# Receptance projection in three fp32r passes, key units from one compact tile, decays taken shifted

## The chip, the cores and the metric

The kernel runs on one core of a Trainium2 chip. The metric is the device time of one execution in microseconds (us); shown are the median, the lowest and the highest of the runs.

## The reference, cut to what matters

The program computes two transformer blocks over 256 tokens of width 1024. The change lies in one stage of the second block, an RWKV-7 time mix with 16 heads of 64:

```python
xx = _token_shift(h) - h
xr, xw, xk, xv, xa, xg = [h + xx * mu[i] for i in range(6)]
r = (xr @ w_r).astype(f32)
k = (xk @ w_k).astype(f32)
v = (xv @ w_v).astype(f32)
w = -jax.nn.softplus(-(w0 + jnp.tanh(xw @ w1) @ w2).astype(f32)) - 0.5
a = jax.nn.sigmoid((a0 + (xa @ a1) @ a2).astype(f32))
g = jax.nn.sigmoid(xg @ g1) @ g2
kk = heads(k * k_k.astype(f32))
kk = kk / jnp.maximum(jnp.sqrt(jnp.sum(kk * kk, axis=-1, keepdims=True)), 1e-12)
k = k * (1.0 + (a - 1.0) * k_a.astype(f32))
decay = jnp.exp(-jnp.exp(w))
...
bonus = jnp.sum(rh * kh * r_k.astype(f32), axis=-1, keepdims=True) * vh
```

## The kernel before

Eight stages run one after the other, four of them feed-forward blocks (ffn) that take most of the span. All weights come as one stream of chunks of 128 x 2048 floats, 256 output columns of a matrix each, through three buffers (`raw`). A chunk is used in one of two ways. A plain chunk is multiplied as it is in fp32, 16 products of 128x256 (`plain_columns`, L986). A split chunk is rounded by ACT (ScalarE) to `whi` (`high`, L314), the rest `wlo` is made by POOL (GpSimd; `low`, L3372), and PE (TensorE) multiplies in three fp32r passes, 48 shorter products (`three_passes`, L341 to L343). The buffer of a plain chunk comes free when PE is done, that of a split chunk when its low part is made.

In the RWKV stage the receptance chunks are `RW(0)` to `RW(3)`, the keys `RW(4)` to `RW(7)`, the values `RW(8)` to `RW(11)`; of the first eight, 5 to 7 are split and the rest plain. DVE (VectorE) makes the six mixed inputs (`mix_tile`, L2534) into two homes, `variant_x[0]` and `[1]`, and the tile `x`. Variant 0 is for the keys, 1 and 2 for the decay and a LoRAs, 3 for the gate LoRA, 4 for the receptance, 5 for the values. Each engine runs its instructions in written order, tied by semaphores.

The order of PE is: keys 4 to 7 with a product that sums the squares of two key tiles behind each (`square_sums`, L2854; its output stands repeated over all 64 rows of a head, and the last one is between two LoRAs); the first halves of the LoRAs (`first`, L2847); their second halves (`second`, L2903), two and two, with the quarters of `RW(0)` between; `RW(1)` to `RW(3)` (L986); the values `RW(8)` (L999), in whose second half the bonus sums (L2928) wait for DVE's product `rk` (L2601); half of `RW(9)`; then the scores (L2962), which wait for the scaled factors. DVE divides the keys by their lengths in four steps (`unit_kk`, L2562 to L2564), then forms key and decay factors: running sums (L2582), a subtraction (L2584) that gives the sums before each token, and from ACT three exponentials (L2409, L2412, L2414).

## Time and profile before

| what | us |
|---|---|
| median of 3 runs | 1230.28 |
| lowest, highest | 1229.87, 1230.87 |
| the profiled execution, its own time | 1229.58 |
| its span | 1227.80 |
| what lies around the span | 1.78 |
| PE busy | 1215.9 |
| POOL, ACT, DVE busy | 778.8, 608.4, 539.5 |

Times in rows are us from the span's start. The RWKV stage lies from about 822 to 1020. An fp32 product stands in the trace as two records, an fp32r product as one. PE products overlap at their ends, so the pace of a row of them is read from start to start and not from the duration of one.

### The profile page before, as it was taken

The page shows a single profiled execution, that of the slowest core. Times are in us where ns is not written, and L with a number is a line of the kernel's source. Part 1 is how long each engine was busy: PE and PEld are TensorE (multiplying, and loading weights), DVE is VectorE, ACT ScalarE, POOL GpSimd, SP SyncE. Part 2 cuts the span into 40 slices and gives each one's busy share as a digit, 9 for nine tenths or more (in the row PEclk, how much of TensorE's full clock was granted, in tenths as well). Part 3 has the DMA queues.
Part 4 walks back from the last instruction along what each step waited for, and adds up shares of the span by engine and source line. Part 5 has one row for each costly group of instructions (what it writes and reads, how often), then busy time and mean ns, then how long its engine had stood idle before and what let it go on. Part 6 is the DMA issues. An engine that isn't in the chain of part 4 may idle for free.

```text
span 1227.8 us, 23237 instructions
## 1 busy us (share of the span) xinstructions
PE 1215.9 (99%) x9698; PEld 1060.6 (86%) x9698; DVE 539.5 (44%) x819; ACT 608.4 (50%) x796; POOL 778.8 (63%) x200
## 2 busy tenths in 40 slices
PE   8999999999999999999999999999999999999998
PEld 7888887788888888899998888888888998888887
DVE  4432234665433333243533332249996574332233
ACT  6544443545464444486465454455421445554443
POOL 3988880154288888766459888853015535888884
PEclk9999999999999999999999999999999999999999
DMA  7655554244255555554244555552342124555551
GB/s 295 212 196 191 185 202 152 74 177 164 78 194 208 177 199 182 194 197 172 94 144 175 204 176 201 180 196 104 119 156 71 37 74 169 179 199 196 181 203 70
DMA packets 31020, 202.01 MB, mean 165 GB/s; under 512 B 3424, under 2 KB 5344, under 8 KB 7392
## 3 DMA queue, kind: packets, MB, share of 16 engines
q1 hardware_dynamic: 28064, 196.63, 45.3%
q10 hardware_dynamic: 2880, 4.26, 1.1%
q8 instruction: 60, 0.98, 0.3%
q14 instruction: 16, 0.13, 0.0%
HBM read 198.79 MB, written 2.10 MB: 164 GB/s over the span
## 4 chain that ended last, share of the span: by engine, by line
PE 95%; POOL 1%; issue 1%; ACT 1%; DVE 1%; DMA 1%; SPq 0%; POOLq 0%; DVEq 0%
PE psum L353 25%; PE psum L355 13%; PE psum L344 10%; PE psum L346 10%; PE psum L345 10%; PE psum L986 6%; PE psum L999 3%; PE psum L2992 2%; PE psum L3008 1%; POOL wlo L3372 1%; PE psum L2847 1%; PE psum L341 1%; PE psum L343 1%; PE psum L342 1%; PE psum L2962 1%
## 5 line engine op out<-in xcount | busy, mean ns | idle before, releaser
L3372 POOL TENSOR_TENSOR wlo<-raw,whi 128x2048 fp32r<-128x2048 f32 x160 | 736.5, 4609 | 282.0 <-ACT whi L314 237.3
L353 PE MATMUL psum<-f_both,whi 128*128 128x512 f32 x1408 | 493.6, 394 | 2.0 <-DVE wlo L699 2.0
L314 ACT ACTIVATE whi<-raw 128x2048 fp32r<-128x2048 f32 x160 | 306.3, 1915 | 217.3 <-PE psum L355 169.5
L355 PE MATMUL psum<-f_both,wlo 128*128 128x256 f32 x1408 | 394.4, 280 | 0.0
L353 PEld LDWEIGHTS psum<-f_both,whi 128*128 128x128 f32 x1408 | 265.1, 188 | 60.9 <-DVE wlo L699 2.6
L355 PEld LDWEIGHTS psum<-f_both,wlo 128*128 128x128 f32 x1408 | 265.2, 188 | 1.5
L344 PE MATMUL psum<-whi,ahi 128*128 128x512 f32 x352 | 137.4, 390 | 0.2 <-POOL wlo L3372 0.2
L346 PE MATMUL psum<-whi,alo 128*128 128x512 f32 x352 | 137.0, 389 | 0.0
L345 PE MATMUL psum<-wlo,ahi 128*128 128x512 f32 x352 | 137.0, 389 | 0.0
L909 DVE TENSOR_TENSOR psum<-psum,arena 128x512 f32<-128x512 f32 x43 | 30.1, 700 | 237.3 <-ACT arena L625 237.2
L925 DVE TENSOR_TENSOR alo<-arena,ahi 128x512 fp32r<-128x512 f32 x44 | 99.6, 2264 | 31.7 <-ACT ahi L858 31.7
L916 DVE TENSOR_TENSOR psum<-psum,arena 128x512 f32<-128x512 f32 x44 | 30.8, 700 | 171.3 <-ACT arena L625 171.3
L344 PE MATMUL psum<-whi,hhi 128*128 128x256 f32 (+1 forms) x328 | 99.8, 304 | 0.8 <-POOL wlo L3372 0.6
L346 PE MATMUL psum<-whi,hlo 128*128 128x256 f32 (+1 forms) x328 | 97.0, 296 | 0.0
L345 PE MATMUL psum<-wlo,hhi 128*128 128x256 f32 (+1 forms) x328 | 96.9, 295 | 0.0
L344 PEld LDWEIGHTS psum<-whi,ahi 128*128 128x128 f32 x352 | 66.1, 188 | 14.3 <-POOL wlo L3372 0.5
L346 PEld LDWEIGHTS psum<-whi,alo 128*128 128x128 f32 x352 | 66.1, 188 | 13.9
L345 PEld LDWEIGHTS psum<-wlo,ahi 128*128 128x128 f32 x352 | 66.1, 188 | 12.1
L986 PE MATMUL psum<-arena,raw 128*128 128x256 f32 x320 | 73.9, 384 | 1.1 <-issue 1.1
L986 PEld LDWEIGHTS psum<-arena,raw 128*128 128x128 f32 x320 | 59.3, 190 | 10.7 <-issue 3.0
L344 PEld LDWEIGHTS psum<-whi,hhi 128*128 128x128 f32 x328 | 61.7, 188 | 5.0 <-issue 1.7
L858 ACT ACTIVATE ahi<-arena 128x512 fp32r<-128x512 f32 x44 | 27.9, 633 | 73.1 <-DVE arena L922 73.1
(425 smaller groups left out, 1506.7 us busy)
## 6 DMA issues: line engine op xcount, KB each, us to landing
raw<-stream SPq DMA_DIRECT2D x182, 1024.0 KB, 4.8
con<-consts SPq DMA_DIRECT2D x1, 1376.0 KB, 14.7
x<-x_in SPq DMA_DIRECT2D x1, 1024.0 KB, 5.1
raw<-stream SPq DMA_DIRECT2D x2, 512.0 KB, 7.5
kept_x<-x ACTq DMA_DIRECT2D x1, 1024.0 KB, 3.9
x<-kept_x ACTq DMA_DIRECT2D x2, 512.0 KB, 4.6
out<-x SPq DMA_DIRECT2D x4, 256.0 KB, 2.0
arena<-gm_w_s ACTq DMA_DIRECT2D x1, 512.0 KB
```

Of the source, the lines that this page charges most:

```text
L314: nc.scalar.activation(whi[:, slot, :], raw[:, c % RAW, :], ACT.Copy).then_inc(high_made, 1)
L344: nc.tensor.matmul(out, h_hi, w_hi, start=start, stop=False, skip_group_check=skip)
L345: nc.tensor.matmul(out, h_hi, w_lo, start=False, stop=False, skip_group_check=skip)
L346: return nc.tensor.matmul(out, h_lo, w_hi, start=False, stop=stop, skip_group_check=skip)
L353: nc.tensor.matmul(psum[:, bank, :].rearrange("p (a n) -> p a n", a=2), whi[w], f_both[:, :, k, :], start=k == 0, stop=False, skip_group_c ...
L355: return nc.tensor.matmul(psum[:, bank, 0:TOK], wlo[w], f_hi[:, k, :], start=False, stop=k == KT - 1, skip_group_check=True)
L909: nc.vector.tensor_tensor(left, left, aside[:, 0, :, :], ALU.add).then_inc(s("ffn_sum"), 1)
L916: nc.vector.tensor_tensor(left, left, aside[:, 1, :, :], ALU.add).then_inc(s("ffn_sum"), 1)
L925: nc.vector.tensor_tensor(flat(alo), act[:, b, :], flat(ahi).bitcast(F32), ALU.subtract)\
L986: mm = nc.tensor.matmul(psum[:, bank, j * 256:(j + 1) * 256], raw[:, slot, k * 256 + j * P:k * 256 + j * P + P], h[:, k, :], start=k == 0, ...
L999: mm = nc.tensor.matmul(psum[:, bank, m * 256:m * 256 + n], h[:, k, m * P:m * P + P], raw[:, slot, k * 256:k * 256 + n], start=k == 0, sto ...
L3372: nc.gpsimd.tensor_tensor(part(wlo[:, slot, :]), part(raw[:, c % RAW, :]), part(whi[:, slot, :]).bitcast(F32), ALU.subtract)\
```

## The change

The receptance chunks 1 to 3 become split chunks: ACT makes `whi` inside its own order (one in the middle of the sigmoids, two behind reads of `RW(0)` and `RW(1)`), DVE makes `wlo` (`receptance_low`), ACT and DVE also split variant 4 (`rx_hi`, `rx_lo`), and PE multiplies in three passes. The square sums are made by eight products with 32 output rows each into one bank (`square_sums`), one root, one clamp and one reciprocal follow, and eight products over 32 rows each spread the result (`spread_units`, behind `RW(1)`); DVE multiplies all keys in one instruction. Variants 1 and 2 are multiplied together, 64 output rows each (`first_pair`), variant 3 goes to the tile `x`. The subtraction and the first exponential go: the factor before each token is read one token to the left in the exponential of the running sums, within chunks of 64. The factor `r_k` moves from DVE's product into the weights of the bonus sums.

```diff
-RWKV_SPLIT = [("rw", 0, j) for j in (5, 6, 7)]
+RWKV_SPLIT = [("rw", 0, j) for j in (5, 6, 7, 1, 2, 3)]
...
+            rx_hi = below.enter_context(nc.sbuf_tensor("rx_hi", [P, KT, TOK], F32R))
...
+            rx_lo = below.enter_context(nc.sbuf_tensor("rx_lo", [P, KT, TOK], F32R))
...
-        mixed_x = lambda v: value_x if v == 5 else variant_x[v % 2]
+        mixed_x = lambda v: value_x if v in (3, 5) else variant_x[v % 2]
...
+        of_head = s3m[:, 256:384]
+        bonus_weights = s3m[:, 384:400].rearrange("p (k h) -> p k h", k=8)
...
+        def home_free(eng, v):
+            if v == 2:
+                eng.wait_ge(chunk_used, USE[CH[RW(4)]] + 1)
+                eng.wait_ge(s("rw_mixed"), 12)
+            if v == 3:
+                eng.wait_ge(s("x_kept"), 16)
+            if v >= 4:
+                eng.wait_ge(s("rw_first"), v - 2)
...
-            root(3)
+            eng.wait_ge(s("rw_sums"), 1)
+            nc.scalar.activation(roots[:, 0:2, :], bank2(2), ACT.Sqrt).then_inc(s("rw_root"), 1)
             eng.wait_ge(s("rw_first"), 2)
             nc.scalar.activation(lw[0:64, 0, :], psum[0:64, 0, 0:256], ACT.Tanh).then_inc(s("rw_lw"), 1)
             nc.scalar.activation(lw[64:128, 0, :], psum[64:128, 0, 256:512], ACT.Copy).then_inc(s("rw_lw"), 1)
+            for b in range(4):
+                k = slice(2 * b, 2 * b + 2)
+                eng.wait_ge(s("rw_mixed"), mixed(4, 2 * b + 1))
+                nc.scalar.activation(rx_hi[:, k, :], variant_x[0][:, k, :], ACT.Copy).then_inc(s("rw_rhi"), 1)
...
+                if k == 4:
+                    highs.upto(CH[RW(1)])
...
-                eng.wait_ge(s("rw_kx"), 4)
                 read(nc.scalar.activation(rr[:, 2 * j:2 * j + 2, :], bank2(proj_bank(name)), ACT.Copy), name)
-                if j == 0:
+                if j < 2:
+                    highs.upto(CH[RW(2 + j)])
+                if j == 1:
                     eng.wait_ge(s("rw_before"), 1)
-                    nc.scalar.activation(sw, sw, ACT.Exp, scale=-DECAY).then_inc(s("rw_exp"), 1)
-                if j == 1:
-                    eng.wait_ge(s("rw_before"), 2)
                     nc.scalar.activation(sw, sums, ACT.Exp, scale=DECAY).then_inc(s("rw_exp"), 1)
-                    eng.wait_ge(s("rw_exp"), 2)
+                    eng.wait_ge(s("rw_exp"), 1)
                     nc.scalar.activation(sums, sums, ACT.Exp, scale=-DECAY).then_inc(s("rw_exp"), 1)
...
+            for h in range(2):
+                steps(nc.vector.tensor_copy(of_head[:, 64 * h:64 * h + 64], const("block_ident", 32)[:, 16 * h:16 * h + 1].broadcast_to((P, 64))))
+            r_k = vec[:, VEC_AT["r_k"]:VEC_AT["r_k"] + 8].rearrange("p (k a) -> p k a", a=1).broadcast_to((P, 8, 2))
+            heads = const("same64")[:, 0:P:64].rearrange("p (a h) -> p a h", a=1).broadcast_to((P, 8, 2))
+            steps(nc.vector.tensor_tensor(bonus_weights, r_k, heads, ALU.mult))
...
+            for v in range(1, 5):
+                mix_variant(v)
+            eng.wait_ge(s("rw_root"), 1)
+            steps(nc.vector.tensor_scalar(roots[:, 0:2, :], roots[:, 0:2, :], 1e-12, None, ALU.max))
+            nc.vector.reciprocal(roots[:, 0:2, :], roots[:, 0:2, :]).then_inc(s("rw_unit"), 1)
+            mix_variant(5)
+            def receptance_low(j):
+                c = CH[RW(j)]
+                eng.wait_ge(high_made, LOWS[c] - 2)
+                eng.wait_ge(low_made, LOWS[c] - 1)
+                nc.vector.tensor_tensor(wlo[:, SLOT[c], :], raw[:, c % RAW, :], whi[:, SLOT[c], :].bitcast(F32), ALU.subtract)\
+                    .then_inc(low_made, 1)
+            for b in range(4):
                 k = slice(2 * b, 2 * b + 2)
-                eng.wait_ge(s("rw_kk"), 2 * b + 2)
-                steps(nc.vector.tensor_scalar(roots[:, k, :], roots[:, k, :], 1e-12, None, ALU.max))
-                steps(nc.vector.reciprocal(roots[:, k, :], roots[:, k, :]))
-                steps(nc.vector.tensor_tensor(kk[:, k, :], kk[:, k, :], roots[:, k, :], ALU.mult))
-            mix_variant(1)
-            unit_kk(0)
-            for v in (2, 3, 4):
-                mix_variant(v)
-            for b in range(1, 4):
-                unit_kk(b)
+                eng.wait_ge(s("rw_rhi"), b + 1)
+                nc.vector.tensor_tensor(rx_lo[:, k, :], variant_x[0][:, k, :], rx_hi[:, k, :].bitcast(F32), ALU.subtract)\
+                    .then_inc(s("rw_rlo"), 1)
+            receptance_low(1)
             eng.wait_ge(s("rw_sig"), 16)
             for k in range(8):
-                ins = nc.vector.tensor_scalar(rr[:, k, :], aa[:, k, :], 1.0, V_AT("k_a", k), ALU.subtract, ALU.mult)
+                ins = nc.vector.tensor_scalar(sums[:, k, :], aa[:, k, :], 1.0, V_AT("k_a", k), ALU.subtract, ALU.mult)
             steps(ins)
             for j in range(4):
                 k = slice(2 * j, 2 * j + 2)
-                nc.vector.scalar_tensor_tensor(out=kx[:, k, :], in0=rr[:, k, :], scalar=1.0, in1=kx[:, k, :],
+                nc.vector.scalar_tensor_tensor(out=kx[:, k, :], in0=sums[:, k, :], scalar=1.0, in1=kx[:, k, :],
                                                op0=ALU.add, op1=ALU.mult).then_inc(s("rw_kx"), 1)
+            receptance_low(2)
+            receptance_low(3)
+            eng.wait_ge(s("rw_kx"), 4)
             for k in range(8):
                 ins = nc.vector.tensor_tensor_scan(sums[:, k, :], const("restart", TOK), sw[:, k, :], 0.0, ALU.mult, ALU.add)
-            steps(ins)
-            nc.vector.tensor_tensor(sw, sums, sw, ALU.subtract).then_inc(s("rw_before"), 1)
+            ins.then_inc(s("rw_before"), 1)
             eng.wait_ge(S["rw_lw"], 6)
             nc.vector.tensor_tensor(gm_lo, lw[:, 1, :], gm_hi.bitcast(F32), ALU.subtract).then_inc(s("rw_lwlo"), 1)
             nc.vector.tensor_tensor(gt[64:96], lw[64:96, 2, :], gt[64:96].bitcast(F32), ALU.subtract).then_inc(S["rw_lwlo"], 1)
+            eng.wait_ge(s("rw_sums"), 2)
+            eng.wait_ge(s("rw_kk"), 8)
+            kk_halves = kk.rearrange("p (i g) t -> p i g t", i=2)
+            steps(nc.vector.tensor_tensor(kk_halves, kk_halves, psum[:, 2:6, :].rearrange("p g (i t) -> p i g t", i=2), ALU.mult))
             steps(nc.vector.tensor_tensor(aa, aa, kk, ALU.mult))
-            eng.wait_ge(s("rw_exp"), 1)
-            nc.vector.scalar_tensor_tensor(out=kk, in0=kk, scalar=-1.0, in1=sw, op0=ALU.mult, op1=ALU.mult).then_inc(s("rw_before"), 1)
-            eng.wait_ge(s("x_kept"), 16)
-            mix_variant(5)
+            chunks_of = lambda v: v.rearrange("p k (c t) -> p (k c) t", c=4)
             eng.wait_ge(s("rw_exp"), 2)
+            nc.vector.tensor_scalar(chunks_of(kk)[:, :, 0:1], chunks_of(kk)[:, :, 0:1], -1.0, None, ALU.mult)
+            steps(nc.vector.scalar_tensor_tensor(out=chunks_of(kk)[:, :, 1:64], in0=chunks_of(kk)[:, :, 1:64], scalar=-1.0,
+                                                 in1=chunks_of(sums)[:, :, 0:63], op0=ALU.mult, op1=ALU.mult))
             steps(nc.vector.tensor_tensor(aa, aa, sw, ALU.mult))
             for j in range(0, 4):
                 eng.wait_ge(bank_read[proj_bank(RW(j))], PROJ[RW(j)] // 2 + 1)
             eng.wait_ge(s("rw_kx"), 4)
             eng.wait_ge(s("rw_mixed"), mixed(5, 7))
-            for k in range(8):
-                nc.vector.scalar_tensor_tensor(out=rk[:, k, :], in0=rr[:, k, :], scalar=V_AT("r_k", k), in1=kx[:, k, :],
-                                               op0=ALU.mult, op1=ALU.mult).then_inc(s("rw_rk"), 1)
+            for k in (slice(0, 4), slice(4, 8)):
+                nc.vector.tensor_tensor(rk[:, k, :], rr[:, k, :], kx[:, k, :], ALU.mult).then_inc(s("rw_rk"), 4)
             eng.wait_ge(s("rw_rk"), 8)
             steps(nc.vector.tensor_tensor(kx, kx, sw, ALU.mult))
-            eng.wait_ge(s("rw_exp"), 3)
             steps(nc.vector.tensor_tensor(rr, rr, sums, ALU.mult))
             nc.vector.tensor_copy(pc, sums.rearrange("p k (c t) -> p k c t", c=4)[:, :, :, 63]).then_inc(s("rw_scaled"), 1)
...
+            def first_pair():
+                plain_loaded(eng, L0)
+                for k in range(KT):
+                    for v, h in ((1, 0), (2, 1)):
+                        eng.wait_ge(s("rw_mixed"), mixed(v, k))
+                        mm = nc.tensor.matmul(psum[head_rows(h), 0, h * 256:h * 256 + 256], raw[:, L0 % RAW, k * 256 + 64 * h:k * 256 + 64 * h + 64],
+                                              variant_x[v % 2][:, k, :], start=k == 0, stop=k == KT - 1)
+                return mm
+            def square_sums():
+                eng.wait_ge(s("rw_sq"), 8)
+                for half in range(2):
+                    for g in range(4):
+                        mm = nc.tensor.matmul(psum[32 * g:32 * g + 32, 2, half * 256:half * 256 + 256], const("same64")[:, 0:P:4],
+                                              roots[:, 4 * half + g, :], start=True, stop=True)
+                mm.then_inc(s("rw_sums"), 1)
+            def spread_units():
+                eng.wait_ge(s("rw_unit"), 1)
+                eng.wait_ge(s("rw_sig"), 16)
+                for half in range(2):
+                    for g in range(4):
+                        rows = slice(32 * g, 32 * g + 32)
+                        mm = nc.tensor.matmul(bank2(2 + g)[:, half, :], of_head[rows], roots[rows, half, :], start=True, stop=True)
+                mm.then_inc(s("rw_sums"), 1)
...
-            def split_by_tiles(slot, bank):
+            def split_by_tiles(slot, bank, h_hi=key_hi, h_lo=key_lo, made=lambda k: eng.wait_ge(s("rw_mixed"), 8 + k // 2 + 1)):
                 for k in range(KT):
-                    eng.wait_ge(s("rw_mixed"), 8 + k // 2 + 1)
+                    made(k)
                     for j in range(2):
                         w = (slice(None), slot, slice(k * 256 + j * P, k * 256 + j * P + P))
-                        mm = three_passes(bank2(bank)[:, j, :], whi[w], wlo[w], key_hi[:, k, :], key_lo[:, k, :], True,
+                        mm = three_passes(bank2(bank)[:, j, :], whi[w], wlo[w], h_hi[:, k, :], h_lo[:, k, :], True,
...
-                if j:
-                    square_sums(j - 1)
-            eng.wait_ge(s("rw_root"), 1)
-            first(1, 0, 0, L0, 0, P, 256).then_inc(s("rw_first"), 1)
-            square_sums(3)
-            first(2, 0, 1, L0, 0, P, 256).then_inc(s("rw_first"), 1)
-            eng.wait_ge(s("rw_root"), 2)
+            first_pair().then_inc(s("rw_first"), 2)
+            square_sums()
             first(3, 1, 0, L0, P, P, 256).then_inc(chunk_used, 1)
             first(3, 1, 1, L1, D, 96, 96).then_inc(s("rw_first"), 1)
             eng.wait_ge(s("rw_lw"), 2)
-            eng.wait_ge(s("rw_root"), 4)
+            eng.wait_ge(s("rw_root"), 1)
...
-                project(eng, RW(j), plain_columns, h=variant_x[0])
+                project(eng, RW(j), split_by_tiles, h_hi=rx_hi, h_lo=rx_lo, made=lambda k: eng.wait_ge(s("rw_rlo"), k // 2 + 1))
+                if j == 1:
+                    spread_units()
...
-                                          const("same64")[:, 0:P:64], start=True, stop=True)
+                                          bonus_weights[:, k, :], start=True, stop=True)
...
-                    elif c not in PLAIN and names[c] not in (("lora", 0, 2), ("rw_o", 0, 1)):
+                    elif c not in PLAIN and names[c] not in (("lora", 0, 2), ("rw_o", 0, 1), RW(1), RW(2), RW(3)):```

On PE, from the last key chunk to the LoRAs' second halves, before (L2854 square sums, L2847 `first`, L2903 `second`):

```order
L2854 MATMUL psum<-arena,con 128x512 [waits rw_sq]
L2847 MATMUL psum<-arena,raw 128x256 [waits rw_mixed,raw_loaded0,rw_root]
L2847 MATMUL psum<-arena,raw 128x256 [waits rw_mixed] x7
L2854 MATMUL psum<-arena,con 128x512 [waits rw_sq]
L2847 MATMUL psum<-arena,raw 128x256 [waits rw_mixed,raw_loaded0]
L2847 MATMUL psum<-arena,raw 128x256 [waits rw_mixed] x7
L2847 MATMUL psum<-arena,raw 128x256 [waits rw_mixed,raw_loaded0,rw_root]
L2847 MATMUL psum<-arena,raw 128x256 [waits rw_mixed] x7
```

And now (L2877 `first_pair`, L2886 `square_sums`, L2866 `first`):

```order
L2877 MATMUL psum<-arena,raw 64x256 [waits rw_mixed,raw_loaded0]
L2877 MATMUL psum<-arena,raw 64x256 [waits rw_mixed] x15
L2886 MATMUL psum<-arena,con 32x256 [waits rw_sq]
L2886 MATMUL psum<-arena,con 32x256 x7
L2866 MATMUL psum<-x,raw 128x256 [waits rw_mixed,raw_loaded0]
```

The sixteen full-width products of variants 1 and 2 have become sixteen half-width ones, and the four square sums (the first two stand ahead of these rows, behind `RW(5)` and `RW(6)`) one group of eight.

On DVE, from the sums of the decays to the product for the bonus, before:

```order
L2579 SCALAR_TENSOR_TENSOR arena<-arena 128x512 x3
L2582 SCALAR_TENSOR_TENSOR arena<-con,arena 128x256 x8
L2584 TENSOR_TENSOR arena<-arena 128x2048 [waits dve_step]
L2586 TENSOR_TENSOR alo<-arena,ahi 128x256 [waits rw_lw]
L2587 TENSOR_TENSOR ahi<-arena,ahi 32x256
L2589 TENSOR_TENSOR arena<-arena 128x2048
L2591 SCALAR_TENSOR_TENSOR arena<-arena 128x2048 [waits rw_exp,dve_step]
L2534 SCALAR_TENSOR_TENSOR x<-arena,vec 128x256 [waits rw_first,x_kept]
L2534 SCALAR_TENSOR_TENSOR x<-arena,vec 128x256 x7
L2595 TENSOR_TENSOR arena<-arena 128x2048 [waits rw_exp]
L2601 SCALAR_TENSOR_TENSOR arena<-arena,vec 128x256 [waits bank_read6,bank_read7,rw_kx,rw_mixed,dve_step]
```

And now (L2579 is `receptance_low`, L2609 the keys times their units, L2622 the product for the bonus):

```order
L2579 TENSOR_TENSOR wlo<-raw,whi 128x2048 [waits low_made,high_made] x2
L2600 SCALAR_TENSOR_TENSOR arena<-con,arena 128x256 [waits rw_kx]
L2600 SCALAR_TENSOR_TENSOR arena<-con,arena 128x256 x7
L2603 TENSOR_TENSOR alo<-arena,ahi 128x256 [waits rw_lw]
L2604 TENSOR_TENSOR ahi<-arena,ahi 32x256
L2609 TENSOR_TENSOR arena<-arena,psum 128x2048 [waits rw_kk,rw_sums]
L2610 TENSOR_TENSOR arena<-arena 128x2048 [waits dve_step]
L2613 TENSOR_SCALAR arena<-arena 128x32 [waits rw_exp,dve_step]
L2614 SCALAR_TENSOR_TENSOR arena<-arena 128x32x63
L2616 TENSOR_TENSOR arena<-arena 128x2048 [waits dve_step]
L2622 TENSOR_TENSOR arena<-arena 128x1024 [waits bank_read7,bank_read6,rw_kx,rw_mixed,dve_step]
```

The running sums now stand behind two low parts of receptance chunks, and the mixing of the values has moved out to a place ahead of them.

On ACT, where the receptance is read, now (L2413 reads a projection, L317 is `high`, L2418 and L2420 the exponentials):

```order
L2413 ACTIVATE arena<-psum 128x512 [waits chunk_used]
L317 ACTIVATE whi<-raw 128x2048 [waits chunk_used,raw_loaded1]
L2413 ACTIVATE arena<-psum 128x512 [waits chunk_used]
L317 ACTIVATE whi<-raw 128x2048 [waits chunk_used,raw_loaded2]
L2418 ACT_TABLE_LOAD
L2418 ACTIVATE arena<-arena 128x2048 [waits rw_before]
L2420 ACTIVATE arena<-arena 128x2048 [waits rw_exp]
L2413 ACTIVATE arena<-psum 128x512 [waits chunk_used] x2
```

The high part of `RW(3)` stands behind the read of `RW(1)`, and the reads of `RW(2)` and `RW(3)` behind both exponentials.

## Rows read from the trace of the kernel before

**Rows 1.** The page: busy time of PE; the chain that ended last, by engine.

```profile
PE 1215.9 (99%) x9698; PEld 1060.6 (86%) x9698; DVE 539.5 (44%) x819; ACT 608.4 (50%) x796; POOL 778.8 (63%) x200
PE 95%; POOL 1%; issue 1%; ACT 1%; DVE 1%; DMA 1%; SPq 0%; POOLq 0%; DVEq 0%
```

**Rows 2.** Waits of PE, 822 to 1000: total us, times, longest; the longest.

```profile
PE psum L613 <- DVE arena L468: 0.6, 1, 0.6
```

**Rows 3.** Timeline, PE, 840 to 905: start, us, what, idle before.

```profile
840.55 1.02 PE L2854 MATMUL psum<-arena,con 128*128 128x512 f32 x2
841.16 0.19 PEld L341 LDWEIGHTS psum<-key_hi,whi 128*128 128x128 f32 x1 [0.42 <-POOL wlo L3372]
...
853.54 1.02 PE L2854 MATMUL psum<-arena,con 128*128 128x512 f32 x2
854.40 3.62 PE L2847 MATMUL psum<-arena,raw 128*128 128x256 f32 x16
...
858.71 10.52 PE L2847 MATMUL psum<-arena,raw 128*128 128x256 f32 x48
869.16 2.00 PE L2903 MATMUL psum<-arena,raw 64*128 64x256 f32 x16
...
876.67 24.44 PE L986 MATMUL psum<-arena,raw 128*128 128x256 f32 x112
900.95 3.64 PE L999 MATMUL psum<-raw,x 128*128 128x256 f32 x16
904.42 0.50 PE L2928 MATMUL psum<-con,arena 128*128 128x2 f32 x4
```

**Rows 4.** Timeline, PE, mix1 stage: products narrower than 128, side by side.

```profile
241.06 0.75 PE L1705 MATMUL psum<-arena 32*32 32x32 f32 x64
...
308.80 1.97 PE L1779 MATMUL psum<-arena 128*64 128x128 f32 x32
```

**Rows 5.** Timeline, DVE, 836 to 903.

```profile
836.17 11.97 DVE L2534 SCALAR_TENSOR_TENSOR arena<-arena,vec 128x256 f32<-128x256 f32 x8
...
883.90 4.76 DVE L2582 TENSOR_TENSOR_SCAN arena<-con,arena 128x256 f32<-128x256 f32 x8
888.70 2.29 DVE L2584 TENSOR_TENSOR arena<-arena 128x2048 f32<-128x2048 f32 x1
...
896.34 3.25 DVE L2534 SCALAR_TENSOR_TENSOR x<-arena,vec 128x256 f32<-128x256 f32 x8
...
902.07 3.25 DVE L2601 SCALAR_TENSOR_TENSOR arena<-arena,vec 128x256 f32<-128x256 f32 x8 [0.28 <-DVE arena L2595]
```

**Rows 6.** Groups by line and shape, DVE: count, busy us, mean ns.

```profile
L1417 DVE TENSOR_TENSOR hlo<-arena,hhi 128x2048 fp32r<-128x2048 f32 x1 | 2.2, 2248 | 0.0
...
L1519 DVE TENSOR_TENSOR arena<-arena 128x1024 f32<-128x1024 f32 x1 | 1.2, 1226 | 0.0
```

**Rows 7.** Timeline, ACT, 853 to 902.

```profile
853.74 0.84 ACT L2375 ACTIVATE arena<-psum,vec 128x256 f32<-128x256 f32 x2 [3.95 <-PE psum L343]
...
870.58 0.46 ACT L2399 ACTIVATE arena<-psum,vec 128x256 f32<-128x256 f32 x1
...
873.08 0.51 ACT L2400 ACTIVATE arena<-psum,vec 128x256 f32<-128x256 f32 x1
...
901.15 0.60 ACT L2406 ACTIVATE arena<-psum 128x512 f32<-128x512 f32 x1 [0.35 <-PE psum L986]
901.64 1.90 ACT L314 ACTIVATE whi<-raw 128x2048 fp32r<-128x2048 f32 x1
```

**Rows 8.** DMA issues: count, KB each, us from issue to landing.

```profile
raw<-stream SPq DMA_DIRECT2D x182, 1024.0 KB, 4.8
```

**Rows 9.** Timeline, PE, and the clock by window (stretch, its length, busy (x), PEclk, DMA, GB/s).

```profile
10.73 0.50 PE L353 MATMUL psum<-f_both,whi 128*128 128x512 f32 x1 [1.99 <-DVE wlo L699]
...
12.00:14.00 2.00, 2.00 (x8) 0.52 1.02 431
14.00:16.00 2.00, 2.00 (x9) 0.63 1.02 436
```

More of the change, by code:

```diff
@@ L2362, in rwkv_scalar @@
             highs.upto(CH[RW(7)])
-            def root(b):
-                eng.wait_ge(s("rw_sums"), b + 1)
-                nc.scalar.activation(roots[:, 2 * b:2 * b + 2, :], bank2(b), ACT.Sqrt).then_inc(s("rw_root"), 1)
             for j in range(4):
@@ L2847, in first @@
                     mm = nc.tensor.matmul(psum[0:width, bank, half * 256:half * 256 + 256],
-                                          raw[:, c % RAW, at + k * stride:at + k * stride + width], variant_x[v % 2][:, k, :],
+                                          raw[:, c % RAW, at + k * stride:at + k * stride + width], mixed_x(v)[:, k, :],
                                           start=k == 0, stop=k == KT - 1)
                 return mm
-            def square_sums(b):
-                eng.wait_ge(s("rw_sq"), 4 + b + 1)
-                nc.tensor.matmul(psum[:, b, :], const("same64"), roots[:, 2 * b:2 * b + 2, :], start=True, stop=True)\
-                    .then_inc(s("rw_sums"), 1)
+            def first_pair():
[21 more added lines that the diff above has]
+                mm.then_inc(s("rw_sums"), 1)
             def made(v):
@@ L3121, in y_late @@
                 mm.then_inc(s("rw_late_sum"), 1)
-            eng.wait_ge(s("rw_root"), 4)
             eng.wait_ge(s("rw_scaled"), 2)
@@ L3396, in _ @@
                         rwkv_pool(pool, low)
-                    elif c not in PLAIN and names[c] not in (("lora", 0, 2), ("rw_o", 0, 1)):
+                    elif c not in PLAIN and names[c] not in (("lora", 0, 2), ("rw_o", 0, 1), RW(1), RW(2), RW(3)):
                         low(c)
```

15 lines of the change are left out of this document (3 added, 12 removed).

## The prediction

> **What bounds the kernel now.** I read the page first [rows 1]: PE is busy for 99% of the span, and 95% of the chain that ended last is PE. Then the waits of PE in the RWKV stage [rows 2]: the longest is 0.6 us, so here a microsecond less on PE is a microsecond less on the clock, as long as the others follow. The timelines of PE, DVE and ACT [rows 3, 5, 7] say how closely they follow. The row to see is the start of the first bonus sum, 904.42 [rows 3]: DVE's product for the bonus began at 902.07, its first tile of eight 0.41 later [rows 5], so DVE was ahead by only 1.9. I carry a schedule forward from 841 to that point; behind it the program's order and lengths are as before, and what is gained there moves the end.
>
> **PE, part by part.** An fp32 chunk takes 6.94: 56 products in 900.95 - 876.67 = 24.28, 0.434 each, times 16 [rows 3]. A split chunk takes 5.64: two of them and one square sum of 0.86 (853.54 to 854.40) fill 841.41 (840.55 + 0.86) to 853.54 [rows 3]. Three chunks save 3 x 1.30 = 3.9. Four square sums cost 4 x 0.86 = 3.4. The first saves next to nothing: behind it the weight load of `RW(6)` waited 0.42 for POOL until 841.16 [rows 3], and POOL's low part is not moved. So keys 6 start at 841.25 instead of 841.41 and keys 7 end at 852.5.
>
> `first_pair`: products of 64 output rows, in turn on either half. The trace has that form: L1779, 16 products of 128 columns (32 records) in 1.97, 0.123 each, where one alone would take half of 0.434 [rows 4]. So two run side by side, and the sixteen take 8 x 0.434 + 0.1 = 3.6 against 6.94: until 856.2. Variant 1 is ready at 848.1 [rows 5] and variant 2 a mix of 3.25 later, 851.4, so it doesn't wait.
>
> The new square sums and `spread_units` are eight products of 256 columns each, on four strips. The trace has no such form. Alone they would take 8 x 0.434 = 3.5. The nearest row is L1705, 32 products of 32x32 in 0.75, 0.023 each, where one alone takes 0.054 (an eighth of 0.434): at least 2.3 run side by side [rows 4]. Bounds per group: 0.87 (all four together) to 3.5; I take 1.05, near the lower, since that row is held back by its very short products. The sums are made by 857.3.
>
> The Trainium skill (TensorEngine Tiling (Array Packing), Tiling Modes) lists 128x32 and 32x128 as four tiles that operate independently, and says that a change of mode drains the engine; by that page a group would be 0.87 and a drain. That a drain costs little the trace shows: L1779's 16 products take at most 0.23 more than eight pairs of 0.217 would [rows 4].
>
> Then two `first` of 6.94 end at 864.25 (variant 3 is ready at 854.7), `second` 1.93 and the first half of `RW(0)` 3.65, the other `second` 1.93, the second half 3.47: `RW(0)` ends at 875.3, against 880.14 before [rows 3]. The sigmoids began 1.42 behind the last `first` (870.58, 869.16) and come 0.357 apart (eight in 870.58 to 873.08 and one more) [rows 3, 7]. Now they begin at 865.7; ACT puts the high part of `RW(1)`, 1.92, behind the eighth, at 868.6; the last eight begin with the second `second`, 871.0, and end at 873.9.
>
> **The low parts.** A low part of 128x2048 on DVE is 2.25 [rows 6], the high part on ACT 1.92 [rows 7]. `RW(1)`: variant 5 is mixed by 867.7, the four `rx_lo`, 2048 columns in four pieces, take 2.4 (as above, rows 6), the low part follows the high part's end and runs 870.55 to 872.85, ahead of 875.3. `RW(1)` then ends at 881.0. `RW(2)`: its buffer comes free with the last `second` at 871.8; the load lands 4.8 later [rows 8], high part 876.85 to 878.8, low part to 881.1, and PE wants it at 882.1 after `spread_units`. A full microsecond of slack. `RW(3)`: ACT reads `RW(1)` first. From the end on PE to ACT 0.2 (853.54 to 853.74), 0.49 until ACT goes on (901.15 to 901.64), 1.92 for the high part [rows 3, 7]: 883.65; low part until 886.0, ahead of 887.9. PE ends `RW(3)` at 893.5, against 900.95: 7.45 earlier.
>
> **Who is late next.** DVE comes to the running sums only behind that low part, at 886.0. From the start of these sums to the product `rk` the old order took 902.07 - 883.90 = 18.17 [rows 5]. Of that the mix of the values goes, 3.2, and the subtraction, 2.2 of pace; what comes is the keys times their units, 2048 elements read from PSUM, bounded by 2.25 (a 128x2048 row) and 2.45 (two of 128x1024) [rows 6]; no row of that size reads PSUM, and I take 2.3, like the fp32 row from SBUF [rows 5]; and the first columns of the chunks, 0.15 to 0.3. The shifted product has the size of the one before. That gives 15.2: 901.3. The first half of `rk`, 128x1024, is 1.23 [rows 6]: 902.6 with the signal to PE. So the bonus sums start at 902.6 against 904.42: **1.8 saved**, not 7.45. The chain is: `RW(1)` ends on PE, read, high part, low part, sums, products, 21.6 in all; PE needs for `spread_units`, two chunks and half of `RW(8)` (3.47) only 15.9. ACT shows the same: the exponentials come 890.8 to 894.6, the read of `RW(2)` behind them ends at 895.2, and `RW(8)` needs that bank. So PE waits 1.7 ahead of `RW(8)` and **3.9 ahead of the bonus sums**.
>
> Hidden: the longer ACT list (three high parts 5.8, four `rx_hi` of 0.6, less one exponential) lies in ACT's waits. If it didn't, each part of it ahead of the high part of `RW(3)` would be paid in full. The three clamps and reciprocals that go from DVE stood ahead of the sigmoids' end, and so off the chain.
>
> **The clock.** In the old trace the granted clock is at full speed all through this stage. After the wait of 1.99 near the start it fell to the half (1.2 GHz): 0.52 of full from 12 to 14, 0.63 from 14 to 16, full again after that [rows 9]. What was lost is 2 x 0.48 + 2 x 0.37 = 1.7. A wait of 3.9, with one of 1.7 shortly ahead, is longer than that, and I expect the same. Part of the slow stretch may fall into the wait and cost nothing, so the cost is 0.7 to 1.7; I take 1.4. The net is 1.8 - 1.4 = 0.4.
>
> The Trainium skill (TensorE: Matmul & The Clock Gate, What's actually happening) says that the throttled clock is the default and that activity releases it. That is the rule that speaks against this change, and the fall near the start agrees.
>
> **The sum.** The profiled execution before is 1229.58, span 1227.80 and 1.78 around it; 0.70 under the median. Minus 0.45: 1229.1 for a profiled one, and 1230.28 - 0.45 = **1229.8** as the median.
>
> **The rivals.**
> - The clock holds. For: full clock in all waits up to 0.6. Against: rows 9. Time: 1230.28 - 1.85 = 1228.4.
> - The thirty-two-row products don't run side by side: slower than before. The first group then costs 3.5, 2.4 more, ahead of `RW(1)` and so on the chain; it decides from about 0.4 more on, where the net gain is gone. 1229.8 + 2.4 = 1232.2. For: no row has the form. Against: L1705.
> - DVE isn't late, since its products or the low parts are shorter than the rows say, and PE's own sum counts: 1230.28 - 7.45 = 1222.8. Against: every term has a row.
> - The change doesn't do what it says: a low part or a load of a receptance chunk comes behind PE's need. `RW(2)` is the close one, with a slack of 1.0, and the chain through `RW(3)` has 2.6 of slack there on DVE; 1 to 2 late gives 1229.8 to 1231.
>
> **How the numbers follow.** Forecast with the clock falling 0.57 (1229.2 to 1230.8), clock holding 0.20, strips in turn 0.10, DVE not late 0.05, late chunk 0.08. A measurement of this kernel tells apart about 0.2%, 2.46: faster means under 1227.8, slower over 1232.7. Faster: 0.05 from the PE sum, 0.07 of the holding clock (its chain is uncertain by some 0.7), 0.02 of the rest: 0.14. Slower: 0.04 of the strips, 0.04 of a late chunk or a longer slow stretch: 0.08. Range 1227.6 to 1232.2.
>
> **What would show it.** Right: a three-pass `RW(1)` of about 5.6; first bonus sum near 902.6; PE waits there 3 to 4, released by DVE's `rk`, and 1 to 2 ahead of `RW(8)`, released by ACT; a window behind 898 with a clock near the half. Both groups of strips near 1.05. Wrong: no wait of PE at the bonus sums; a wait ahead of `RW(1)` or `RW(2)`; a square-sum group of 3.5; a low part on DVE well over 2.3.

## The result, and the profile after

| | before | after |
|---|---|---|
| median, us | 1230.28 | 1236.27 |
| lowest, highest | 1229.43, 1230.98 | 1235.27, 1237.86 |
| the profiled execution's span | 1227.8 | 1233.8 |
| mean granted clock of PE | 0.998 | 0.993 |

Five runs of either. The ratio is 1.0053, with a 95% interval of 1.0041 to 1.0065: slower by 0.5%, and outside the forecast of 1229.8 (1227.6 to 1232.2).

The waits of PE in the RWKV stage, 822 to 1000 (total us, times, longest), where before had nothing over 0.6 [rows 2]:

```profile
PE psum L2968 <- DVE arena L2622: 3.3, 1, 3.3
PE psum L1002 <- issue: 1.2, 1, 1.2
```

These are the two waits that the prediction names, at the bonus sums and ahead of `RW(8)`. The chain that ended last says the same: PE has 93% of it instead of 95% [rows 1], DVE 3% instead of 1%:

```profile
PE 93%; DVE 3%; POOL 2%; issue 1%; ACT 1%; DMA 1%; SPq 0%; POOLq 0%; DVEq 0%
```

PE's timeline from `RW(8)` on (start us, us, what, idle before), beside [rows 3]:

```profile
894.17 3.69 PE L1002 MATMUL psum<-raw,x 128*128 128x256 f32 x16 [1.23 <-issue]
901.20 0.98 PE L2968 MATMUL psum<-arena 128*128 128x2 f32 x4 [3.33 <-DVE arena L2622]
902.04 1.20 PE L1002 MATMUL psum<-raw,x 128*128 128x256 f32 x2
903.03 0.85 PE L2968 MATMUL psum<-arena 128*128 128x2 f32 x4
903.74 1.20 PE L1002 MATMUL psum<-raw,x 128*128 128x256 f32 x2
...
913.98 6.27 PE L1002 MATMUL psum<-raw,x 128*128 128x256 f32 x18
920.18 1.98 PE L3002 MATMUL psum<-arena 64*64 64x128 f32 x64
```

One product of the values (two records) with the bonus sums of one tile (four records of two columns) takes 1.71 (902.04 to 903.74); at the full clock it takes 0.88, as the experiment with constants shows. The last eighteen records take 6.2 instead of some 4.1. The windows show the clock (window, its length, busy us and instructions of PE, PEld, DVE, ACT, POOL, granted clock, DMA share, GB/s):

```profile
898.00:902.00 4.00, 0.81 (x4) 0.81 (x5) 3.91 (x3) 0.00 (x0) 0.00 (x0) 0.91 0.00 0
902.00:906.00 4.00, 4.00 (x14) 3.57 (x15) 3.93 (x3) 0.00 (x0) 0.00 (x0) 0.50 0.00 0
906.00:910.00 4.00, 4.00 (x16) 3.53 (x14) 1.12 (x2) 0.00 (x0) 0.00 (x0) 0.50 0.00 0
910.00:914.00 4.00, 4.00 (x18) 3.64 (x16) 0.00 (x0) 0.00 (x0) 0.00 (x0) 0.50 0.00 0
914.00:918.00 4.00, 4.00 (x11) 3.19 (x12) 3.76 (x6) 0.00 (x0) 1.15 (x1) 0.50 0.39 125
918.00:922.00 4.00, 4.00 (x74) 3.37 (x72) 0.86 (x2) 0.00 (x0) 2.63 (x2) 0.96 0.92 350
```

PE is busy in every microsecond from 902 to 918, and runs at the half clock (1.2 GHz) in all of them. The stretch near the start that the prediction took as its measure lasted less than 4 [rows 9].

DVE is late, but by no more than was forecast (DVE, timeline; in this execution the stage begins 1.0 earlier than in that of before, with the first three-pass product of the keys at 833.71 against 834.74, so forecasts are to be moved by that):

```profile
882.72 2.29 DVE L2579 TENSOR_TENSOR wlo<-raw,whi 128x2048 fp32r<-128x2048 f32 x1 [1.49 <-ACT whi L317]
884.93 4.77 DVE L2600 TENSOR_TENSOR_SCAN arena<-con,arena 128x256 f32<-128x256 f32 x8
...
890.49 2.29 DVE L2609 TENSOR_TENSOR arena<-arena,psum 128x2048 f32<-128x2048 f32 x1
...
899.91 2.36 DVE L2622 TENSOR_TENSOR arena<-arena 128x1024 f32<-128x1024 f32 x2
```

**The balance.** Moved by 1.0, before would have its first bonus sum at 903.4; after has it at 901.20: 2.2 gained. From there to the scores (L3002) after takes 920.18 - 901.20 = 18.98. Before, the same work took 915.00 - 904.42 = 10.58 [rows 3]; its scores in PE's timeline:

```profile
910.93 4.13 PE L999 MATMUL psum<-raw,x 128*128 128x256 f32 x18
915.00 1.98 PE L2962 MATMUL psum<-arena 64*64 64x128 f32 x64
```

So 8.4 are lost, 6.2 net; the medians differ by 5.99. The two spans differ by 6.0 and the starts of their scores by 5.2: behind the scores this execution loses another 0.8 against that of before, which nothing here assigns.

### The profile page after: what moved, and what is told of

Same layout as the page of the kernel before. It is cut to its first block, busy times and chain, and to the rows that moved or that the text cites. A ratio compares the mean times of both kernels' runs of the same rounds, so it can differ in the third digit from the quotient of the medians.

```text
span 1233.8 us, 23376 instructions
## 1 busy us (share of the span) xinstructions
PE 1216.5 (99%) x9770; PEld 1061.5 (86%) x9770; DVE 529.9 (43%) x814; ACT 612.9 (50%) x799; POOL 779.1 (63%) x200
## 4 chain that ended last, share of the span: by engine, by line
PE 93%; DVE 3%; POOL 2%; issue 1%; ACT 1%; DMA 1%; SPq 0%; POOLq 0%; DVEq 0%
PE psum L356 25%; PE psum L358 13%; PE psum L347 10%; PE psum L349 10%; PE psum L348 10%; PE psum L989 4%; PE psum L1002 3%; PE psum L3032 2%; POOL wlo L3411 2%; PE psum L3048 1%; PE psum L344 1%; PE psum L346 1%; PE psum L345 1%; PE psum L3002 1%; PE psum L602 1%
## 5 line engine op out<-in xcount | busy, mean ns | idle before, releaser
L317 ACT ACTIVATE whi<-raw 128x2048 fp32r<-128x2048 f32 x163 | 312.2, 1916 | 219.2 <-PE psum L358 169.3
L928 DVE TENSOR_TENSOR alo<-arena,ahi 128x512 fp32r<-128x512 f32 x44 | 95.3, 2165 | 31.7 <-ACT ahi L861 31.7
L348 PEld LDWEIGHTS psum<-wlo,hhi 128*128 128x128 f32 x328 | 62.0, 189 | 1.7
L349 PEld LDWEIGHTS psum<-whi,hlo 128*128 128x128 f32 x328 | 61.7, 188 | 1.8
## 6 DMA issues: line engine op xcount, KB each, us to landing
raw<-stream SPq DMA_DIRECT2D x182, 1024.0 KB, 4.8
x<-x_in SPq DMA_DIRECT2D x1, 1024.0 KB, 5.0
kept_x<-x ACTq DMA_DIRECT2D x1, 1024.0 KB, 3.9
```

The source lines that it names most:

```text
L317: nc.scalar.activation(whi[:, slot, :], raw[:, c % RAW, :], ACT.Copy).then_inc(high_made, 1)
L348: nc.tensor.matmul(out, h_hi, w_lo, start=False, stop=False, skip_group_check=skip)
L349: return nc.tensor.matmul(out, h_lo, w_hi, start=False, stop=stop, skip_group_check=skip)
L928: nc.vector.tensor_tensor(flat(alo), act[:, b, :], flat(ahi).bitcast(F32), ALU.subtract)\
```

## The experiments

Each time is a median with the lowest and the highest beside it, each ratio is to the kernel before, which ran beside them: its median was 1230.18 beside the kernels with ten constants, DVE late, one block and plain chunks, and 1229.9 beside the others.

**Constant products in the waits.** Three products of constants ahead of `RW(8)` and seven ahead of the first bonus sum keep PE busy and compute nothing that is used.

```diff
+                if k == 0:
+                    idle_constants(7, 0)
                 eng.wait_ge(s("rw_rk"), k + 1)
...
+            idle_constants(3, 0)
             project(eng, RW(8), plain_tokens, h=value_x, wait=made(5), between=bonus_sums)
```

> The changed kernel with three constant fp32 products of 128x256 ahead of the values' first chunk and seven (3.0 us) ahead of the first bonus sum, so that PE works where it waited 1.2 and 3.3; nothing else is altered. Theory clock (the wait makes the granted clock fall, and the stretch behind it runs at half): the clock stays at 1.0, the stretch from the first bonus sum to the first scores takes 10.6 as in the kernel before and not 19.0, time 1227.5 to 1228.5. Rival work (the stretch is long because of its own products: new weights for the bonus sums, DVE's long products beside it): the stretch stays near 19, time about 1236.

Measured: 1228.21 (1227.28 to 1229.18), ratio 0.9983 (0.9973 to 0.9992). PE's timeline:

```profile
898.42 3.19 PE L391 MATMUL psum<-con 128*128 128x256 f32 x14
901.91 0.61 PE L2970 MATMUL psum<-arena 128*128 128x2 f32 x4 [0.30 <-DVE arena L2622]
902.38 0.68 PE L1002 MATMUL psum<-raw,x 128*128 128x256 f32 x2
902.89 0.50 PE L2970 MATMUL psum<-arena 128*128 128x2 f32 x4
903.26 0.68 PE L1002 MATMUL psum<-raw,x 128*128 128x256 f32 x2
...
912.59 1.98 PE L3005 MATMUL psum<-arena 64*64 64x128 f32 x64
```

The first bonus sum comes even 0.7 later than in after, but the pace behind it is 0.88 instead of 1.71, the stretch to the scores takes 912.59 - 901.91 = 10.68 as in before, and the program is 1236.27 - 1228.21 = 8.1 faster. Nothing else is changed, so the rival, that the stretch is long because of its own products, is out. Ten products whose results nobody reads are worth 8.1 us, net of the 0.7 that they cost: the price of the clock is some 8.8 by the medians and 8.4 by the two timelines above. The change with the constants in gains 2.0.

**Part of the waits filled.** Only three constants, ahead of the first bonus sum.

```diff
+                if k == 0:
+                    idle_constants(3, 0)
                 eng.wait_ge(s("rw_rk"), k + 1)
```

> The changed kernel with only three constant products (1.3 us) ahead of the first bonus sum and none ahead of the values' first chunk: PE then waits 1.2 there and about 2.0 at the bonus sums. It asks how long a wait it takes. If the fall needs the whole 3.3: clock 1.0 and 1228.2 like the run with ten products. If a wait of 2.0, as the one near the start of the program, is enough: the slow stretch of about 17 is back, 1236; in part of the executions, between these.

Measured: 1235.24 (1227.52 to 1237.14, 5 runs), ratio 1.0026 (0.9998 to 1.0054). A wait of 2.0 is left. Four of the five executions have a mean clock of 0.992 to 0.996 and 1232.9 to 1237.1; one has 1.000 and 1227.52. So a wait of 2.0 here fells the clock in most executions, not in all, and one execution can differ from the next by 8 through that alone. In the profiled one (1236.41) the wait ends at 902.22, the clock is still 1.00 from 902 to 904, and it is 0.64 from 904 to 906: it fell some 2 us behind the wait, with PE in the mix of long and short products.

**Before, with DVE late.** To the kernel before, three DVE products whose results nobody uses are added ahead of `rk`, and nothing else is changed.

```diff
+            steps(nc.vector.tensor_tensor(roots, sw, sw, ALU.mult))
+            steps(nc.vector.tensor_tensor(roots, sw, sw, ALU.mult))
+            steps(nc.vector.tensor_tensor(roots[:, 0:2, :], sw[:, 0:2, :], sw[:, 0:2, :], ALU.mult))
             for k in range(8):
                 nc.vector.scalar_tensor_tensor(out=rk[:, k, :], in0=rr[:, k, :], scalar=V_AT("r_k", k)
```

> The kernel before with three more DVE products into an unused area (2.3, 2.3 and 0.7 us) ahead of the product for the bonus, so that PE waits about 3.3 there with everything else as before. Theory clock: the clock falls and stays at half until the bonus sums are over, the stretch to the scores takes about 19 instead of 10.6: 1230.3 + 3.3 + 8.4 = 1242. Rival work: only the wait is added, 1233.6.

Measured: 1240.79 (1239.79 to 1241.24), ratio 1.0083 (1.0066 to 1.01).

```profile
907.32 0.61 PE L2931 MATMUL psum<-con,arena 128*128 128x2 f32 x4 [3.40 <-DVE arena L2604]
...
919.20 5.08 PE L999 MATMUL psum<-raw,x 128*128 128x256 f32 x16
```

Its windows, over the same stretch:

```profile
910.00:914.00 4.00, 4.00 (x17) 3.64 (x15) 3.93 (x3) 0.00 (x0) 0.00 (x0) 0.50 0.00 0
914.00:918.00 4.00, 4.00 (x15) 3.61 (x15) 0.88 (x2) 0.00 (x0) 0.00 (x0) 0.50 0.00 0
918.00:922.00 4.00, 4.00 (x13) 3.31 (x12) 2.58 (x4) 0.00 (x0) 0.00 (x0) 0.50 0.21 27
922.00:924.00 2.00, 2.00 (x11) 1.77 (x10) 1.40 (x3) 0.00 (x0) 1.93 (x2) 1.00 0.87 360
```

A wait of 3.4 costs 10.6 here: itself and some 7 of clock, for a slow stretch of some 14 us (0.59 from 908 to 910, 0.50 until 922). No three-pass chunk stands in this kernel's receptance, so the slow stretch belongs to the place and the wait, not to the new products. It has no wait ahead of `RW(8)` either, so the first of after's two waits isn't needed for it.

**The bonus sums in one block.** The wait stays where it was; the 32 small products stand behind `RW(8)` instead of between its products.

```diff
-            project(eng, RW(8), plain_tokens, h=value_x, wait=made(5), between=bonus_sums)
+            project(eng, RW(8), plain_tokens, h=value_x, wait=made(5), between=after_first)
+            for k in range(KT):
+                bonus_sums(1, k)
```

> The changed kernel with the same wait for the bonus product ahead of the second half of the values' first chunk, but the bonus sums, 32 records of two columns, stand in one block behind that chunk instead of between its products. Theory mix (the clock stays down as long as full products and two-column products alternate): it comes back within about 4 us of full products, the stretch to the first scores takes 12 to 13, time 1229 to 1231. Rival length (a fall of that kind lasts about 17 us whatever follows): the stretch takes 17 to 19, time 1234 to 1236. If the block of small products lowers the clock again, it shows behind it.

Measured: 1232.29 (1227.45 to 1234.8), ratio 1.001 (0.9997 to 1.0024).

```profile
902.35 5.23 PE L1002 MATMUL psum<-raw,x 128*128 128x256 f32 x16 [3.33 <-DVE arena L2622]
907.41 3.63 PE L2968 MATMUL psum<-arena 128*128 128x2 f32 x32
```

```profile
902.00:904.00 2.00, 1.65 (x4) 1.39 (x5) 1.97 (x3) 0.00 (x0) 0.00 (x0) 0.50 0.00 0
904.00:906.00 2.00, 2.00 (x7) 1.62 (x7) 1.97 (x2) 0.00 (x0) 0.00 (x0) 0.64 0.00 0
906.00:908.00 2.00, 2.00 (x15) 1.82 (x13) 2.00 (x1) 0.00 (x0) 0.00 (x0) 1.00 0.00 0
...
912.00:914.00 2.00, 2.00 (x8) 1.56 (x6) 1.96 (x3) 0.00 (x0) 0.23 (x1) 0.56 0.04 8
```

Behind the same wait of 3.33 the clock is back by 906 once only full products follow. So the length of the stretch depends on what PE does in it: with small products in between it lasted 14 to 17 us. But behind the block of small products comes a second fall, at 912, with PE busy all the time, and this execution (1234.1) has a third between 1008 and 1012. That is why the median lies above the 1229 to 1231 expected of the mix; it lies below the 1234 of the rival. In this kernel's ten executions the time runs from 1227.45 (clock 1.000) to 1234.8 (0.994), so no fall is certain.

**Three plain chunks, or two, or one.** `RW(1)` to `RW(3)` in fp32 again, the rest of the change kept; then with `RW(1)` alone in three passes, and with `RW(1)` and `RW(2)`. The edits are of one kind; the one with two chunks:

```diff
-RWKV_SPLIT = [("rw", 0, j) for j in (5, 6, 7, 1, 2, 3)]
+RWKV_SPLIT = [("rw", 0, j) for j in (5, 6, 7, 1, 2)]
...
             receptance_low(2)
-            receptance_low(3)
...
+                if j == 3:
+                    project(eng, RW(j), plain_columns, h=variant_x[0])
```

> The changed kernel without its first part: receptance chunks 1 to 3 stay plain fp32, no high and low parts of them or of their input; compact units, paired LoRA products, shifted decays stay. Theory chain (the three low parts on DVE make it late, so PE waits, so the clock falls): no wait ahead of the bonus sums, clock 1.0 throughout, PE's saving of square sums and pair counts in full less spread_units, 4.9 - 1.1 = 3.8: 1226.5. Rival: the lateness comes from the compact units (a late product of all keys) and stays: a wait of 2 or more and a slow stretch, over 1230.

> The changed kernel with receptance chunk 1 alone in three passes, chunks 2 and 3 plain. DVE is ready early; against the kernel with all three plain PE saves one chunk's 1.3 and nothing else: 1226.9 - 1.3 = 1225.6, clock 1.0. Rival: a three-pass chunk gives less than 1.3 on the clock, since its weight loads or its low part cost as much elsewhere: 1226.9.

> The changed kernel with receptance chunks 1 and 2 in three passes and chunk 3 plain. DVE's running sums begin one low part and one wait for it earlier, at about 881 instead of 885, PE needs 1.3 longer for chunk 3. Theory chain: no wait at the bonus sums, first one near 897.6 in the changed kernel's own times, scores 5.8 earlier than in the kernel before, 1224.4. Rival: DVE is still late by over 1 us, since the chain begins with the low part of chunk 2, which waits for the load: a wait of 1 to 2, clock as it may be, 1226 to 1231.

| chunks in three passes | median (lowest to highest) | ratio (95%) | first bonus sum, wait ahead, profiled execution |
|---|---|---|---|
| none | 1226.91 (1225.42 to 1228.36) | 0.9971 (0.9962 to 0.9981) | 900.40, none |
| one | 1225.32 (1224.42 to 1226.89) | 0.9964 (0.9951 to 0.9976) | 899.31, none |
| two | 1224.63 (1223.76 to 1228.85) | 0.9954 (0.9937 to 0.9971) | 899.06, none |
| three (after) | 1236.27 (1235.27 to 1237.86) | 1.0053 (1.0041 to 1.0065) | 901.20, 3.33 |

The kernels with none, one and two chunks came within 0.5 of what was expected. With all chunks plain the compact units and their late product of all keys are still there, and no wait is: it takes the low parts on DVE and the shorter products on PE to make one.

The kernel with two was run again, beside the last two experiments:

> The kernel with RW(1) and RW(2) in three passes once more, on the same chip as the two with POOL: 1224.6 as the first time, with single executions up to 1228.9 where the clock falls for some 6 us near 1001 in the last chain of the state (0.50 from 1002 to 1006 in its profile). The kernel with POOL should be 0.8 ahead of it: three chunks save 1.3 more than two, less 0.6 of wait for POOL's low part.

Measured: 1225.01 (1223.76 to 1225.7), ratio 0.9955 (0.9942 to 0.9968). This is the lowest median, 5 under before. The parts without three-pass receptance bring 3.3, the first chunk 0.9 to 1.6, the second 0.3 to 1.2 (by ratios or by medians; the intervals of one and two chunks overlap, so the gain of the second isn't clear of noise), and the third costs 11 to 12. It costs so much since DVE is then late: PE's products get shorter and DVE's list longer, and PE has the wait at the worst place.

The highest of the two-chunk kernel, 1228.85, is the profiled one, and shows a second place of this sort, in the last chain of the state:

```profile
998.00:1000.00 2.00, 1.30 (x46) 1.22 (x42) 1.80 (x4) 1.27 (x3) 0.00 (x0) 1.00 0.00 0
1000.00:1002.00 2.00, 2.00 (x53) 1.90 (x49) 1.89 (x4) 0.00 (x0) 0.00 (x0) 0.73 0.03 8
1002.00:1004.00 2.00, 2.00 (x5) 1.16 (x4) 0.30 (x1) 0.00 (x0) 0.00 (x0) 0.50 0.57 86
1004.00:1006.00 2.00, 2.00 (x34) 1.86 (x33) 0.00 (x0) 0.00 (x0) 0.00 (x0) 0.50 0.94 393
1006.00:1008.00 2.00, 2.00 (x8) 1.21 (x10) 1.79 (x3) 1.78 (x3) 0.00 (x0) 0.56 0.98 410
```

A wait of 0.7 there, among products of 64x64, is followed by some 7 us at half speed, in this execution and not in the three others that ran with it (clock 1.000, 1223.76 to 1224.7). The slow stretch is worth at most 3.4 of the 4 to 5 by which it stands above them. The profiled executions of the kernel with one block (0.50 and 0.69 from 1008 to 1012) and of the first kernel with POOL below (0.50 from 1012 to 1018) have it too. No run changes anything there, so what brings it isn't shown.

**The bonus sums later.** They go into the first half of `RW(9)`, which gives DVE 3.5 more.

```diff
-            project(eng, RW(8), plain_tokens, h=value_x, wait=made(5), between=bonus_sums)
+            project(eng, RW(8), plain_tokens, h=value_x, wait=made(5))
...
+                mm = plain_tokens(c % RAW, proj_bank(RW(8 + j)), value_x, parts=(part,),
+                                  between=(lambda m, k: bonus_sums(1, k)) if (j, part) in ((1, 0), (1, 1)) else None)
```

> The changed kernel with the bonus sums between the products of the first half of the values' second chunk instead of the second half of the first: PE has 3.5 us of ready products where it waited 3.3. Theory (DVE's chain late at one place, and the clock behind it): no wait over 0.5 at the bonus sums, clock 1.0, scores begin about 5.5 earlier than in the kernel before, 1224.7. Rival (what is taken from that wait comes back as a wait of the scores for DVE's scaled factors): a wait of 2 to 3 ahead of the scores, 1227 or more with the clock falling there.

Measured: 1227.47 (1226.22 to 1228.69), ratio 0.998 (0.9969 to 0.999): 2.8 above what I expected. The wait at the bonus sums is gone and the clock holds there, but a new wait has come. DVE, then PE:

```profile
908.26 0.19 DVE L2643 COPY arena<-psum 128x32 f32<-128x32 f32 x1 [0.89 <-PE psum L2968]
...
913.57 1.72 DVE L2682 TENSOR_TENSOR arena<-con,arena 128x512 f32<-128x512 f32 x1
915.32 0.71 DVE L2673 STREAM_TRANSPOSE arena<-arena 128x512 f32<-128x512 f32 x1
```

```profile
916.09 1.15 PE L3033 MATMUL psum<-arena 64*64 64x64 f32 x32 [1.77 <-DVE arena L2673]
```

The copy of the sums (L2643) stands in DVE's list ahead of the last LoRA's low parts and of the transpose that PE needs next. It waits 0.89 for the moved sums, as long as in before (0.90), but now the scores begin right behind the sums, and PE waits 1.77 for what stands behind the copy. Of that, 1.04 is DVE held up: L2682 took 1.72 instead of the 0.68 of after, while POOL ran two products, 3.78 in all, from 910.96 on; the experiment with POOL below shows the same. The wait is 1.8 of the 2.8. In the profiled execution the clock also fell at the second place (0.51 and 0.64 from 1010 to 1014), which is worth about 1.7 there; it is not in all executions (clock 0.998 to 1.000), so the last microsecond is assigned only in part.

**The low part of `RW(3)` on POOL.** POOL does nothing from 845 to 916 in after, and DVE is what is late.

```diff
             receptance_low(2)
-            receptance_low(3)
...
+                if names[c] == ("rw", 0, 3):
+                    pool.wait_ge(low_made, LOWS[c] - 1)
...
-                    elif c not in PLAIN and names[c] not in (("lora", 0, 2), ("rw_o", 0, 1), RW(1), RW(2), RW(3)):
+                    elif c not in PLAIN and names[c] not in (("lora", 0, 2), ("rw_o", 0, 1), RW(1), RW(2)):
```

> The low part of RW(3) moves from DVE to POOL, which does nothing from 845 to 916 in the changed kernel; all three chunks stay in three passes. If DVE's chain is what makes PE wait, its running sums come behind the low part of RW(2) alone: 881.2 instead of 884.9, 3.7 earlier, and the first product for the bonus is ready at 897.5 instead of 901.2. POOL takes 4.6 for the low part, from 882.7 to 887.3, 0.6 later than PE wants it (886.7), so PE ends RW(3) at 893.4 and reaches the bonus sums at 896.9: a wait of 0.6 ahead of RW(3) and one of 0.6 ahead of the bonus sums, both too short to fell the clock. The first bonus sum then comes 4.4 ahead of that of the kernel with ten constant products (901.9, median 1228.2): 1223.8. The rival, that the clock falls in the bonus sums whatever the length of the wait since three-pass chunks stand ahead of them, gives a slow stretch again and 1223.8 + 8 = 1232.

Measured: 1235.76 (1234.49 to 1239.67), ratio 1.0045 (1.0032 to 1.0058). Twelve above my 1223.8. PE's wait at the bonus sums is 3.33 as before, that ahead of `RW(8)` 1.94. DVE, then POOL, then the running sums by themselves (ns least, median, most; first and last start):

```profile
880.22 2.29 DVE L2579 TENSOR_TENSOR wlo<-raw,whi 128x2048 fp32r<-128x2048 f32 x1 [1.69 <-ACT whi L317]
882.43 9.12 DVE L2599 TENSOR_TENSOR_SCAN arena<-con,arena 128x256 f32<-128x256 f32 x8
```

```profile
883.39 4.70 POOL L3412 TENSOR_TENSOR wlo<-raw,whi 128x2048 fp32r<-128x2048 f32 x1 [37.93 <-ACT whi L317]
```

```profile
L2599 DVE TENSOR_TENSOR_SCAN arena<-con,arena x8: 656/659/5031, 882.4 to 890.9; 128x256 f32<-128x256 f32 x8
```

The wait that was to shrink to 0.6 did not, so the two sides of the expectation weren't told apart. The running sums do start 2.5 earlier than in after, but one of the eight takes 5.03 instead of 0.66: it stands while POOL's product of 4.70 runs, and the eight take 9.12 instead of 4.77. What leaves DVE's list comes back as a stop of DVE. The trace of before had shown it: the mix of 11.97 [rows 5], the same eight instructions that take 3.25 elsewhere [rows 5], ran from 836.17 on, when POOL made two low parts (836.40, 9.47). I had read that row for its end only. The Trainium skill (SBUF — State Buffer, the section on the two separate sides) says that DVE and GpSimd share one pair of ports, held by one of them for its whole instruction while the other "fully blocks", when the DVE instruction has two inputs in SBUF and the GpSimd instruction reads SBUF, as here. The 5.03 beside the 4.70 agrees, and so does the kernel with the bonus sums later: beside the same POOL products L2682, with both inputs in SBUF, took 1.72, and L2681 just ahead of it, with one in PSUM, 0.69.

> As the kernel with the low part of RW(3) on POOL, with three constant products ahead of the first bonus sum (1.3 of work, which may cost up to 0.7 more than the wait that it fills). If the wait of 0.6 is harmless, this is 0 to 0.7 slower: 1223.8 to 1224.5. If some executions of the kernel without them lose the clock there, this one loses it in fewer, and its highest time lies below the other's.

The diff adds the three constants of above to it. Measured: 1236.71 (1228.18 to 1238.76), ratio 1.0043 (1.0026 to 1.006); the wait is still 2.04, and two of twelve executions keep the clock (1228.18 and 1228.35). A miss for the same reason.

## Why the prediction was wrong, point by point

- **Chunks, `first_pair`, strips: right.** `first_pair` took 3.6 (851.59 to 855.20), as forecast. The square sums took 1.03 (855.20 to 856.23) and `spread_units` 1.10 (880.18 to 881.28), against 1.05: the four strips run side by side, and the rival in which they go in turn is out. `RW(1)` in three passes took 5.97 up to `spread_units`, 0.3 over the 5.64. `RW(1)` began at 874.2, where `RW(0)` was forecast to end at 874.3 (875.3 less the 1.0 by which this execution is early).
- **Low parts in time: right.** Less 1.0, those of `RW(1)`, `RW(2)` and `RW(3)` were forecast to start at 869.55, 877.8 and 882.65, and started at 869.59, 878.93 and 882.72. `RW(2)` is 1.1 late, since its load landed later (ACT waited until 876.98), and that slack of 1.0 was just used up: PE waited for none of the three by more than 0.4. The rival "late chunk" did not decide.
- **Who is late next: right.** The first bonus sum came at 901.20, forecast 902.6 - 1.0 = 901.6; the waits are 3.33 (forecast 3.9) and 1.23 (1.7). The product with PSUM took 2.29 (2.3).
- **The clock: right that it falls, wrong in what it costs.** This is the step that failed: "What was lost is 2 x 0.48 + 2 x 0.37 = 1.7 ... I expect the same ... I take 1.4". The term measured 8.4 from the two timelines, and 8.1 is what the constants give back after their own cost. I had carried the length of the slow stretch over from the start of the program [rows 9], where long products follow each other. Behind the bonus wait PE has two-column products between the long ones, and there the clock stayed at the half for 17 us; with full products behind a wait of 3.33, in the kernel with one block, it was back by 906. The sum with the measured 2.2 and 8.4 in place of 1.8 and 1.4 is 1230.28 - 2.2 + 8.4 = 1236.5, against the measured 1236.27. The 1.7 was also clock and not time: in after, whose clock did not fall near the start, the first product of `f_both` with `whi` starts at 10.30 (before: 10.73) and the 41st at 26.22 (before: 26.74), so by 27 us the fall had cost 0.1.
- **The rivals and the range.** "The clock holds" was put at 1228.4, and the kernel with ten constants, in which it does, has 1228.21, 0.7 of it the constants' own cost; its price is right within 1, and it isn't what happens. A "longer slow stretch" stood in the chances for slower, in a part of 0.04 shared with the late chunk, with no time worked out for it. It ought to have been the rival on the other side.

Left open: why the block of small products lowers the clock in some executions and not in others, the same for the second place near 1001, and whether the short products behind the wait have a part in the fall itself and not only in its length. With full products behind the wait two of ten executions had a mean clock of 0.999 or more, with the mix none of fourteen.

## What to carry to other kernels

Where PE is the bound and another engine is close behind it, a shorter PE list makes a wait, and the wait's price is its length plus the clock. Read what PE runs behind the wait: if it is a mix of long and very short products, count the whole of that stretch at the half clock, as it was here. Two cheap ways out are shown here, constant products in the wait (8.1 back) and one chunk less (11 back). Before giving work to an idle POOL, look in the trace at what a DVE instruction takes while POOL runs.
